# Beginning the second attention ahead of the input map's last product, in a two-block network on one core

## The reference

```python
h = rms_norm_2(x, pre_mix_g[l])
proj = h @ w_in[l]                     # 1024 x 5376: q, k, v, recurrence, gates
y_a = chunk_band_attention(q, k, v, rel_bias[l])
y_b = rwkv7_time_mix(p_rwkv, ...)
gate_a = jax.nn.sigmoid(p_gate[..., :D_MODEL])
gate_b = jax.nn.sigmoid(p_gate[..., D_MODEL:])
merged = gate_a * (y_a @ proj_a[l]) + gate_b * (y_b @ proj_b[l])
x = x + rms_norm_2(merged @ w_out[l], post_mix_g[l])
```

```python
scores = jnp.einsum('bnqhd,bnkhd->bnhqk', qc, kb) * (d ** -0.5)
scores = jnp.where(valid, scores + bias, NEG_INF)
p = jax.nn.softmax(scores, axis=-1)
out = jnp.einsum('bnhqk,bnkhd->bnqhd', p, vb)
```

## Time and profile before

| what | value |
|---|---|
| median of 3 runs | 3680.86 us (3679.04 to 3688.22) |
| profiled execution | 3670.75 us, its span 3669.0 us |
| granted TensorE clock, mean | 0.933 |
| PE busy | 3484.6 us (95%) |
| VectorE, ScalarE busy | 1969.1 us (54%), 1485.4 us (40%) |
| chain that ended last | PE 88%, DVE 6%, ACT 3%, DMA 1% |
| queue of all DMAs | 344.04 MB, 28.6% of 16 engines |

### The profile page before, as it was taken

One profiled execution on the slowest core, in us unless ns is written; L12 is line 12 of the kernel. 1 busy time (PEld: TensorE's weight loads), 2 busy tenths in 40 slices (PEclk: granted clock), 3 DMA queues, 4 the chain that ended last, 5 costly groups with the idle time before them and its releaser, 6 DMA issues.

```text
span 3669.0 us, 42730 instructions
## 1 busy us (share of the span) xinstructions
PE 3484.6 (95%) x16754; PEld 2714.6 (74%) x16754; DVE 1969.1 (54%) x3296; ACT 1485.4 (40%) x2665; POOL 0.2 (0%) x4
## 2 busy tenths in 40 slices
PE   8978999899999999999989999898898999999998
PEld 7445666688888878888866668787783688888787
DVE  4335666467656555655544336556543366544454
ACT  2033555553333344533433224444431255554443
POOL 0000000000000000000000000000000000000000
PEclk9997999999999999999985559999998999999999
DMA  7310000232222566333340000000004333336665
GB/s 288 130 38 1 1 1 1 81 109 72 86 84 86 166 225 208 111 109 115 102 158 11 8 4 18 18 1 18 1 1 154 125 115 98 115 120 193 229 194 185
DMA packets 249016, 346.76 MB, mean 95 GB/s; under 512 B 11120, under 2 KB 140784, under 8 KB 245616
## 3 DMA queue, kind: packets, MB, share of 16 engines
q1 hardware_dynamic: 248816, 344.04, 28.6%
HBM read 276.88 MB, written 67.11 MB: 94 GB/s over the span
## 4 chain that ended last, share of the span: by engine, by line
PE 88%; DVE 6%; ACT 3%; DMA 1%; issue 1%; SPq 0%; DVEq 0%; ACTq 0%
PE ps L199 86%; PE ps L1207 1%; DVE M L2676 1%; DMA wr<-in_w_down 1%; PE ps L693 1%; DVE NM L1972 0%; DVE QT L1990 0%; DVE RT L1989 0%; PE ps L2369 0%; DVE QT L1992 0%; ACT L2799 0%; DMA kept<-ob 0%; ACT L2797 0%; PE ps L234 0%; ACT M L2621 0%
## 5 line engine op out<-in xcount | busy, mean ns | idle before, releaser
L387 DVE TENSOR_TENSOR wl<-wr,wh 128x512 fp32r<-128x512 f32 x782 | 509.7, 688 | 606.7 <-ACT wh L363 604.0
L363 ACT ACTIVATE wh<-wr 128x512 fp32r<-128x512 f32 x782 | 455.0, 623 | 662.1 <-PE ps L199 538.4
L199 PE MATMUL ps<-ffn_h,wh 128*128 128x512 f32 x2176 | 671.8, 390 | 5.4 <-DVE Y L451 3.9
L199 PEld LDWEIGHTS ps<-ffn_h,wh 128*128 128x128 f32 x2176 | 408.7, 188 | 91.5 <-DVE Y L451 4.7
L199 PE MATMUL ps<-ffn_h,wl 128*128 128x512 f32 x1088 | 423.9, 390 | 0.0
L199 PE MATMUL ps<-in_h,wh 128*128 128x512 f32 x1200 | 369.7, 389 | 2.3 <-DVE Yf L451 1.5
L199 PE MATMUL ps<-wh,wh 128*128 128x512 f32 x864 | 338.2, 391 | 9.7 <-DVE wl L387 9.7
L199 PE MATMUL ps<-wl,wh 128*128 128x512 f32 x864 | 337.5, 391 | 0.0
L199 PE MATMUL ps<-wh,wl 128*128 128x512 f32 x864 | 337.4, 390 | 0.0
L199 PE MATMUL ps<-M,M 128*128 128x128 f32 (+1 forms) x2176 | 297.3, 297 | 37.4 <-DVE ybT L2838 16.6
L199 PEld LDWEIGHTS ps<-M,M 128*128 128x128 f32 (+1 forms) x2176 | 277.9, 203 | 56.7 <-DVE ybT L2838 18.0
(11 more groups left out here) (343 smaller groups left out, 5184.1 us busy)
## 6 DMA issues: line engine op xcount, KB each, us to landing
wr<-hid SPq DMA_DIRECT2D x108, 512.0 KB, 4.0
wr<-in_w_down SPq DMA_DIRECT2D x108, 512.0 KB, 4.7
wr<-in_w_up SPq DMA_DIRECT2D x54, 512.0 KB, 5.4
hid<-ob SPq DMA_DIRECT2D x108, 256.0 KB, 2.3
wr<-in_w_in SPq DMA_DIRECT2D x42, 512.0 KB, 4.9
kept<-ob SPq DMA_DIRECT2D x84, 256.0 KB, 2.0
late<-in_w_ada SPq DMA_DIRECT2D x16, 1024.0 KB, 5.0
wr<-in_w_out SPq DMA_DIRECT2D x32, 512.0 KB, 4.3
```

The source lines that it names most:

```text
L199: return e.op.matmul(out, left, right, start=start, stop=stop, skip_group_check=True)
L363: e.op.activation(self.rows(s)[0], src, ACT.Copy).then_inc(*e.event(self.name + "_act", ("w_high", self.name, s)))
L387: e.op.tensor_tensor(lo, src, hi.bitcast(F32), ALU.subtract).then_inc(*e.event(self.name + "_dve", ("w_low", self.name, s), *done))
```

## The change

The attention's first steps move into the map, ahead of its last product, on PE, ScalarE and VectorE (`before_last`, `first`).

- `QK` and `VT` become single tiles at other places. QK tiles 0 and 4 and VT tile 0 take the three raw buffers; they are reloaded behind p1 of the last pair, when the last weights are split. VT 1 to 3 follow p3, the bias tables of heads 0 and 1 follow the store of the p6 block, the other six QK tiles come behind them. `V` moves to buffers that p7 leaves.
- PE turns VT tile 0 (8 transposes, banks 6 and 7), makes the scores of items 0 and 1, and only then the last product, for which p7 and p4 use bank 4. ScalarE and VectorE copy the turned tile and do the softmax steps of items 0 and 1; VectorE takes the last product's sum behind them.
- VT 1 to 3 are turned at items 1, 2 and 3. The side work starts at item 4 instead of 0.
- The sigmoids of the last two blocks stand behind the side work's first sigmoid, at item 5. SP stores the two blocks then, ahead of `RAW` loads 2 to 4.
- The fences behind the map and the values go. VectorE waits for all stores only behind the attention. SP waits for the last product, not for the end of the map on all engines.

```diff
         for what, i, a in self.work:
+            if (what, i, a) == self.work[-1]:
+                self.before_last(e)
...
-            e.wait_ge(k.bank(group)[1])
+            e.wait_ge(self.free_bank(what, i)[1])
...
             elif what in ("p6", "p7", "p4"):
+                if q == len(self.work) - 1:
+                    self.before_last(e)
                 e.wait_ge(("product", self.name, what, i))
                 self.sums(e, what, i)
...
+
+        assert self.width(0) <= 512 and self.width(1) <= 384
+        for i in (0, 1):
+            parts = scores(i)
+            for n, part in enumerate(parts):
+                self.score_part(e, i, part, n == len(parts) - 1)
+
     def tensor(self, e, scores, extra):
...
-                e.wait_ge(("turned", self.name, self.turns[i, j // 4 * 4]))
+                e.wait_ge(("turned", self.name, self.turns[i, j // 4 * 4]), *self.values_ready(i))
...
-        self.QK = k.sb("QK", [128, 8, 1024], 0)
-        self.VT = k.sb("VT", [128, 4, 1024], 32)
-        self.V = k.sb("V2", [128, 8, 512], 171)
+
+        self.QK = [k.sb("QK", [128, 1024], o) for o in (96, 4, 8, 12, 100, 20, 24, 28)]
+        self.VT = [k.sb("VT", [128, 1024], o) for o in (160, 36, 40, 44)]
+        self.V = k.sb("V2", [128, 8, 512], 64)
+        self.BI = [k.sb(f"BI{i}", [128, 640], 188 + 2.5 * i) for i in range(2)]
 
     def dram(self, m):
...
-    def sync(self, e):
-
-        super().sync(e)
+    def last(self, what, i):
+        return i == self.pairs - 1 and what in ("p7", "p4")
+
+    def free_bank(self, what, i):
+
+        return self.k.settle(self.group(what, i), 4) if self.last(what, i) else super().free_bank(what, i)
+
+    def late_scalar(self, e, what, i):
+
+        if not self.last(what, i):
+            super().late_scalar(e, what, i)
+
+    def last_scalar(self, e):
+        for what in ("p7", "p4"):
+            super().late_scalar(e, what, self.pairs - 1)
+
+    def last_store(self, e):
+        for what in ("p7", "p4"):
+            super().store(e, (what, self.pairs - 1, 0))
 
     def store(self, e, step):
-        super().store(e, step)
+
         what, i, _ = step
-        if (what, i) == ("p3", self.pairs - 1):
-            e.wait_ge(("product", self.name, "p2", i))
-            for h2 in range(4):
-                for m in (h2, 4 + h2):
-                    self.back(e, self.QK[:, m, :], m)
+        if not self.last(what, i):
+            super().store(e, step)
...
+            return
...
+            for m in (0, 4, 8):
+                self.back(e, m, "back0" if m < 8 else "back_v0")
...
             e.wait_ge(("product", self.name, "p3", i))
-            for m in range(4):
-                self.back(e, self.VT[:, m, :], 8 + m)
-
-    def back(self, e, dst, m):
+            for m in (9, 10, 11):
+                self.back(e, m, "back_v")
+        if what == "p6":
+            e.wait_ge(("product", self.name, "p6", i))
+            for h in range(2):
+                self.load_bias(e, h)
+        if what == "p7":
+            for m in (1, 5, 2, 6, 3, 7):
+                self.back(e, m, "back1")
+
+    def back(self, e, m, name):
         e.wait_ge(*self.kept(m))
-        e.op.dma_start(dst, self.k.d["kept"][m, :, :]).then_inc(*e.load(f"back{m % 4}", ("back", m)))
-
-    def values_tensor(self, e):
+        e.op.dma_start((self.QK[m] if m < 8 else self.VT[m - 8])[:, :], self.k.d["kept"][m, :, :]).then_inc(*e.load(name, ("back", m)))
+
+    def load_bias(self, e, h):
+        e.op.dma_start(self.BI[h % 2][:, :], self.k.d["bias"][h, :, :]).then_inc(*e.load(f"bias{h % 2}", ("bias", h)))
+
+    def values_tensor(self, e, m):
 
...
-        for m in range(4):
...
-                e.wait_ge(free, ("back", 8 + m))
-                for j in range(4):
-                    x = e.op.transpose(k.out(group, 128, 128 * j), self.VT[:, m, (4 * g + j) * 128:(4 * g + j + 1) * 128], k.cst("ident"))
...
-    def values_ready(self):
-        return [("read", ("turn_v", m, g)) for m in range(4) for g in range(2)]
+            bank, free = k.settle(group, 6 + g)
+            e.wait_ge(free, ("back", 11 if m else 8))
+            for j in range(4):
+                x = e.op.transpose(k.out(group, 128, 128 * j), self.VT[m][:, (4 * g + j) * 128:(4 * g + j + 1) * 128], k.cst("ident"))
+            x.then_inc(*e.event("in2_mm", ("mm", group)))
+
+    def values_copy(self, e, m):
+        g = 0 if e is self.k.act else 1
+        group = ("turn_v", m, g)
+        e.wait_ge(("mm", group))
+        copy(e, self.V[:, 4 * g:4 * g + 4, m * 128:(m + 1) * 128], self.k.out(group).rearrange("p (u n) -> p u n", u=4)).then_inc(
+            *e.event(f"in2_{e.name}", ("read", group)))
+
+    def values_ready(self, m):
+        return [("read", ("turn_v", m, g)) for g in range(2)]
+
+    def before_last(self, e):
+        self.after.first(e)
 
...
                              [(0, 640), (640, 1280)], [3, 4], 5)
-        self.attend.loaded = lambda i: [("back", self.attend.items[i][0] // 2), ("back", 4 + self.attend.items[i][0] // 2)]
+        self.attend.loaded = lambda i: [("back", 4)] if i < 16 else [("back", 7)]
...
+    def sync(self, e):
+        d, into = self.k.d, self.into
+        e.wait_ge(("product", "in2", "p4", into.pairs - 1), *into.kept(into.tile(into.pairs - 2, 0)))
+        e.op.dma_start(self.SCM[:, :], d["scan"][:, 0:512]).then_inc(*e.load("scan", "scan"))
+        e.op.dma_start(self.WA[0:64, :], d["w2"]).then_inc(*e.load("w2", "w2"))
+        e.op.dma_start(self.WA[64:128, :], d["a2"]).then_inc(*e.load("a2", "a2"))
+        e.op.dma_start(self.WG[:, :], d["g2"]).then_inc(*e.load("g2", "g2"))
+        for n in range(2):
+            self.fetch(e, n)
+        into.last_store(e)
+        for n in range(2, 5):
+            self.fetch(e, n)
+        for h in range(2, 8):
+            e.wait_ge(("biased", "att2", 8 * (h - 2) + 7))
+            into.load_bias(e, h)
+        for n in range(5, 14):
...
+
...
-    def sync(self, e):
-        d = self.k.d
-        e.wait_ge(*[("end", "in2", n) for n in ("pe", "act", "dve")], *self.into.all_stored())
-        e.op.dma_start(self.SCM[:, :], d["scan"][:, 0:512]).then_inc(*e.load("scan", "scan"))
-        for h in range(2):
...
         e.op.activation(self.SG[:, :], self.SG[:, :], ACT.Sigmoid).then_inc(*e.event("mix_act", "gate_hidden"))
+        self.into.last_scalar(e)
         yield
...
                     copy(e, self.yaT[:, c, g * 512:(g + 1) * 512], self.k.out(group)).then_inc(*e.event(f"mix_{e.name}", ("read", group)))
 
+    def first(self, e):
+
+        k, into, attend = self.k, self.into, self.attend
+        if e is k.pe:
+            into.values_tensor(e, 0)
+            e.wait_ge(*[("read", k.tenant[b]) for b in range(3)])
+            attend.first_tensor(e, self.scores)
+        else:
+            into.values_copy(e, 0)
+            for i in range(2):
+                attend.exponential(e, i) if e is k.act else attend.biased(e, i)
+
+    def beside(self, e, begin, values):
+
+        def extra(i):
+            if 1 <= i <= 3:
+                values(e, i)
+            elif i > 3:
+                next(begin, None)
+        return extra
+
     def tensor(self, e):
-        self.into.values_tensor(e)
-        fence(e, "values")
+        e.wait_ge(*[("read", self.k.tenant[b]) for b in range(3, 6)])
         beside = self.begin_tensor(e, 6, 8)
-        self.attend.tensor(e, self.scores, lambda i: next(beside, None))
+        self.attend.tensor(e, self.scores, self.beside(e, beside, self.into.values_tensor))
         together(beside)
         fence(e, "att2")
         heads_tensor(self.k, e, "turn_ya", self.O)
@@ -2866,11 +2922,8 @@
         fence(e, "mixer")
 
     def scalar(self, e):
-        e.wait_ge(*self.into.all_stored())
-        self.into.values_copy(e, 0)
...
     def vector(self, e):
+        e.op.memset(self.STt[:, 0, :], 0.0).then_inc(*e.event("mix_dve", "state_0"))
+        e.wait_ge(*self.into.kept(self.into.tile(self.into.pairs - 2, 1)))
...
-        e.op.memset(self.STt[:, 0, :], 0.0).then_inc(*e.event("mix_dve", "state_0"))
-        self.into.values_copy(e, 1)
-        fence(e, "values")
-        beside = self.begin_vector(e)
-        self.attend.vector(e, lambda i: next(beside, None))
-        together(beside)
         fence(e, "att2")
         self.turn_copies(e, 1)
         fence(e, "ya")
```

More of the change, by code:

```diff
@@ L906, in tensor @@
                 self.product(e, what, i)
+    def free_bank(self, what, i):
+        return self.k.bank(self.group(what, i))
+    def before_last(self, e):
+        pass
     ON_TOP = {"p2": "p1_copied", "p3": "p5_copied", "p4": "p7_read"}
@@ L1250, in order @@
     def order(self, e, soft, values, extra):
-        for i in (0, 1):
-            soft(i)
         for i, turns, ahead in self.beats():
@@ L2190, in __init__ @@
         self.k, self.into = k, into
-        QK, V = into.QK, into.V
-        self.BI = [k.sb(f"BI{i}", [128, 640], 188 + 2.5 * i) for i in range(2)]
+        V, self.BI = into.V, into.BI
```

(1 more changed line is left out.)

94 lines of the change are left out of this document (37 added, 57 removed).

## The result

The changed kernel takes 3535.8 us (median of four, 3534.2 to 3545.1) against 3682.6 us (median of four, 3679.0 to 3688.2): a ratio of 0.9605, with a 95% interval of 0.9584 to 0.9626. I had forecast 3663 us. The profiled execution took 3545.1 us, with a span of 3543.3 and a mean granted clock of 0.965, where it was 0.933 before. The experiments will show that the kernel before has executions of two kinds, some near 3560 and some near 3680 us; the four here were of the second kind alone.

The account below looks back on a forecast made before the run. TensorE was taken as the bound, at the low clock in the second attention. Turn 8 19.9 us earlier, less 1.8 for side matmuls still to come, gave −18 us: 3663 us from the median 3680.86; range 3645 to 3676.

Parts of the forecast that it names:

- Start: From the map's last products to the first turn of P (turn 0): turn 0 at 1886.5, not 1900.9, 14.4 us gained.
- Items 0 to 3: Second attention's first four items, with 24 value transposes added: 10 us at the high clock, 20.2 at the low.
- rival 1: The clock falls at the start, in items 0 to 2; items 0 to 3 take 20.2 us; 3674 us; chance 0.15.
- Items 4 to 7: Items where the side work now starts: 21.5 us, with VectorE standing still some 5.5 us for a reload.
- Turn 8: Turn of item 8, where the second head starts: at 1918.0 against 1937.85, 19.9 us earlier.
- Rival 4: Reloaded operands not there when PE arrives: price 0 to 1 us, 3663 to 3664 us; within the forecast's 0.66.
- rival 3: Early clock fall plus the wait for the first 512-column shift fully on PE: slower, 3683.5 us; chance 0.05.
- Behind turn 8 both run at the low clock with PE as bound: Attention from item 8 on: 36.7 us a head at 0.50 in both kernels, so no gain there.
- Rival 2: The high clock outlives the side work: 3655 us for four more items, 3606 from item 37 on; chance 0.14.

Follow-up runs that it names:

- the variant with the early reload: The changed kernel with the side work's third reload issued on SP ahead of the last two stores: 3543.5, 3646.9, 3650.7 and 3658.8 us.
- the pause: Item 44's exponential done 16 times in place of once, so that TensorE idles: 3698.8 us in the kernel before, 3592.9 us in the changed kernel.
- the variant with six matmuls at item 10: The changed kernel with the third reload ahead of the last two stores and 6 matmuls of 128 rows, 512 columns more at item 10: 3643.6 to 3655.2 us.
- the kernel with the gap: The changed kernel with item 0's exponential done 31 times, so that TensorE idles between the last product and the first turn of P: 3682.2 us.

## Why the prediction was wrong

**Right, by its own steps.** *Start*: turn 0 at 6.9 us behind the map was forecast, 5.9 measured (bias load 3.24 us, taken as 3.8; from the first biased score to turn 0 2.04 us, taken as 2.55 with the table load in it, which now lies in VectorE's wait; the last product starts 1.7 us behind the map, taken as 2.1). *Items 0 to 3*: high clock and 10.1 us forecast, 1.00 and 10.27 measured, so *rival 1* did not occur: eight value turns in each of items 1 to 3 did not take the clock. The Trainium skill, TensorE: Matmul & The Clock Gate, section Part 4 (PE-mode transpose), says that the full clock does not engage for transposes. The traces here do not agree: before the change the clock rose within 32 value turns with nothing else on PE. *Items 4 to 7*: 21.5 forecast, 20.17 measured, with VectorE's standstill 5.03 us for 5.5, and the clock high up to item 6. Turn 8: a gain of 19.9 forecast, 21.9 measured. *Rival 4* and *rival 3* did not occur.

**Wrong.** The step that failed is "Behind turn 8 both run at the low clock with PE as bound". I had read 266 us at 0.50 with PE 100% busy as a property of the attention. It is one of two states. The sum gave this stretch no gain at all (and 1.8 us back for the squares); the runs showed 113.1 us gained there, 840 records at 0.98 in 149.9 us against 837 at 0.50 in 263.0. I took for certain what the few executions at hand showed; in later sets 19 of 35 of the same kernel were lifted.

The sum up to turn 8 was nearly right, and it is close to what remains when both sides are of one kind: 25 us between lifted executions; and 27 us between those that are not lifted, as far as the variant with the early reload may stand for them (median 3650.7 of three, 3677.5 before). Part of the 25 is clock too: in the profile of before's stream that was lifted at 1958.8 the clock was low for 51 us up to the lift, in the two of the changed kernel for 14 and 20. And 3650.7 us is what my 3663 us forecast: the changed kernel without the lift, 12 us better than I had it.

Rival 2 named the mechanism and gave it 0.14, but priced it from item 37 on (57 us) and argued against it with the standstills of items 5 to 7. Those did take the clock, at 1917.3, in the profiled execution (in the second profile it fell without such a wait). Nor is it a second stretch of a few items: the clock was high from item 10 to the end. What I left out is that it could come back: the trace of before has a rise at 1912.6, of which I used only the 10 us behind it, and not the rows ahead of it:

```profile
1908.90 2.08 PE L199 MATMUL ps<-TH,WA 64*128 64x512 f32 x4
1910.77 2.14 PE L199 MATMUL ps<-QK 64*128 64x512 f32 x4
```

These are the side work's decay and rate, on rows 0 to 63 and 64 to 127, so the four records run side by side in pairs: 2.08 us for four, where two scores of this size one behind the other take as long, in the same profile:

```profile
1956.57 2.07 PE L199 MATMUL ps<-QK 64*128 64x512 f32 x2
```

I should have asked what made that rise and where the same work stands after the change. And both counts of before's median, 3 runs and then 4, were of one kind only; two kinds can't be seen in so few.

**What is shown and what is not.** Shown: the 113 us are the clock; the attention alone did not leave 0.50 in any run (98 us of it behind the pause, in both kernels), and kept 1.00 for up to 144 us; a run of matmuls over 128 rows lifts, one over 64 rows in the same place does not (one execution each, and all 31 executions with wide matmuls at item 10 of the kernel before or item 20 of the changed one ended lifted); the same stream is lifted in one execution and not in another; but for the added pause, no run lost the clock for good behind item 15. Argued from the order in time alone: that the squares lift the changed kernel; the rise comes half a microsecond behind them in both of its profiles. Not shown: that the changed kernel's order makes the lift certain. It had it in 8 of 8 executions, in two sets; the kernel before in 19 of 48 (0 of 13 in the first four sets, 19 of 35 in the last two, on other chips); even with the share of the last two sets, 8 of 8 would come up about once in 130. The variants that are one of the two kernels word for word up to item 42 add to both: the changed kernel with the pause was lifted too, and of the eight such executions of the kernel before two were, one on each of two chips where the kernel before had none. An edit of one reload's place brought the changed kernel to 1 of 4. And squares of the same length between the same neighbours lifted in the changed kernel (1920.74 in its second profile) and not in the variant with six matmuls at item 10 (1921.86). Why just this order catches it stays open.

## What to carry to other kernels

When PE is busy all the time at the low clock, don't take that as the stretch's nature: ask whether it would hold the high clock, test it with a few wide matmuls over all 128 rows behind the last long wait, and place work you already have (128 rows, wide, back to back) there. The mix here (scores over 64 rows, values of 64 columns, turns) kept PE busy for 266 us and stayed at 0.50. And where the time can take two values 3% apart, one small edit's effect can be wholly that of which value came up: look at single executions and their mean clock before believing a ratio.

## What the runs showed of the hardware

- 23 us of back-to-back score matmuls with 64 of 128 rows (512 columns, PE busy throughout) left the clock at 0.50; with 128 rows it rose to 1.00 within 2.5 us of their start, and each record took as long, 0.9 us at 0.50.
- The attention ran for 266 us at 0.50 with PE busy in 100% of the time, and for 134 us at 1.00 with PE busy in 98.6%. From turn 8 to the turn of O, 837 records took 263.0 us at 0.50, and 840 took 149.9 us at 0.98.
- The clock rose at 1892 in the trace of before with nothing but transposes on PE, and, by their times, in three executions with 48 of them. In the kernel with the gap it rose just behind twelve, but other matmuls stood ahead of those.
- One wait of 1.35 or 1.36 us, at the same item, was followed by a fall to 0.50 in three profiles and not in three others.
- One and the same kernel took 3551 to 3569 us in 19 and 3671 to 3688 us in 29 of 48 executions, 3% apart, on one core alone.
